# Where the rotated halves of queries and keys come from, and how one projection unit waits for its weights, in a two-layer decoder trunk

## The reference, cut to what matters

```python
for l in range(2):                      # SEQ 256, D_MODEL 1024
    p = rms_norm(x, mix_norm[l]) @ w_in[l]      # columns: RWKV-7 | conv | attention
    y = concat(rwkv7_mix(p_rwkv), short_conv_mix(p_conv), dilated_attention_mix(p_attn))
    x = x + y @ w_o[l]
    x = x + (dense SwiGLU if l == 0 else top-2-of-8 expert SwiGLU)(rms_norm(x))

def rope(x):                            # on normalised queries and keys, 6 heads of 64
    x1, x2 = x[..., :half], x[..., half:]       # half = 32
    return concatenate([x1 * cos - x2 * sin, x2 * cos + x1 * sin])
```

## Time and profile before

| | |
|---|---|
| timed runs | 1595.31, 1606.4 and 1609.2 us; median 1606.4 |
| span of the profiled execution | 1595.9 us; no other time is given for it |
| PE busy | 1563.6 us, 98% |
| DVE busy | 1268.4 us, 79% |
| ACT busy | 1072.2 us, 67% |
| POOL busy | 68.2 us, 4% |
| mean granted clock of PE | 0.995 of full |
| projection of layer 0 and of layer 1 | about 12 to 100 us and 445 to 535 us of the span |

### The profile page before, as it was taken

One profiled execution on the slowest core, in us unless ns is written; L12 is line 12 of the kernel. 1 busy time (PEld: TensorE's weight loads), 2 busy tenths in 40 slices (PEclk: granted clock), 3 DMA queues, 4 the chain that ended last, 5 costly groups with the idle time before them and its releaser, 6 DMA issues.

```text
span 1595.9 us, 29200 instructions
## 1 busy us (share of the span) xinstructions
PE 1563.6 (98%) x11204; PEld 1367.8 (86%) x11204; DVE 1268.4 (79%) x1446; ACT 1072.2 (67%) x1321; POOL 68.2 (4%) x72
## 2 busy tenths in 40 slices
PE   8989999999999999999999999999999999999998
PEld 8978999999999788788888888888888888888886
DVE  5676654544556867899999999999999999999996
ACT  5445354444455454788888888888888888888885
POOL 0012000000000210000100100000100000000000
PEclk9999899999999999999999999999999999999999
DMA  8500555555435006999999999999999999999994
GB/s 311 212 2 4 185 185 185 184 185 183 142 117 183 3 3 246 339 379 370 376 395 370 377 391 367 385 392 365 374 396 371 385 392 364 381 393 368 386 379 162
DMA packets 189562, 446.28 MB, mean 280 GB/s; under 512 B 8080, under 2 KB 10656, under 8 KB 189344
## 3 DMA queue, kind: packets, MB, share of 16 engines
q1 hardware_dynamic: 186480, 434.52, 74.5%
q0 software_dynamic: 2304, 7.87, 2.1%
q10 hardware_dynamic: 688, 2.62, 0.5%
HBM read 438.69 MB, written 6.29 MB: 279 GB/s over the span
## 4 chain that ended last, share of the span: by engine, by line
PE 93%; DVE 4%; ACT 1%; DMA 1%; issue 1%; POOL 0%; SPq 0%; DVEq 0%; ACTq 0%; POOLq 0%
PE bank L767 27%; PE bank L769 27%; PE bank L768 27%; PE bank L748 9%; PE bank L1437 2%; ACT w_hi L1515 1%; PE bank L788 0%; DMA ring<-in_w_in 0%; PE bank L1396 0%; PE bank L1177 0%; DMA ring<-in_dense_wg 0%; PE bank L938 0%; DVE w_lo L2198 0%; DVE ring L2021 0%; DVE w_lo L1945 0%
## 5 line engine op out<-in xcount | busy, mean ns | idle before, releaser
L1515 ACT ACTIVATE w_hi<-ring 128x1024 fp32r<-128x1024 f32 x812 | 858.6, 1061 | 330.9 <-PE bank L769 321.3
L2198 DVE TENSOR_TENSOR w_lo<-ring,w_hi 128x1024 fp32r<-128x1024 f32 x672 | 814.0, 1224 | 67.2 <-ACT w_hi L1515 17.5
L767 PE MATMUL bank<-w_hi,acts_hi 128*128 128x512 f32 (+1 forms) x1376 | 540.4, 393 | 2.3 <-DVE w_lo L2198 2.3
L769 PE MATMUL bank<-w_hi,acts_lo 128*128 128x512 f32 (+1 forms) x1376 | 533.8, 388 | 0.0
L768 PE MATMUL bank<-w_lo,acts_hi 128*128 128x512 f32 (+1 forms) x1376 | 533.2, 387 | 0.0
L767 PEld LDWEIGHTS bank<-w_hi,acts_hi 128*128 128x128 f32 x1376 | 258.8, 188 | 53.8 <-DVE w_lo L2198 3.4
L769 PEld LDWEIGHTS bank<-w_hi,acts_lo 128*128 128x128 f32 x1376 | 258.6, 188 | 53.3
L768 PEld LDWEIGHTS bank<-w_lo,acts_hi 128*128 128x128 f32 x1376 | 259.0, 188 | 50.0
L767 PE MATMUL bank<-acts_hi,w_hi 128*128 128x256 f32 x884 | 254.3, 288 | 3.4 <-DVE acts_lo L2105 1.7
L769 PE MATMUL bank<-acts_hi,w_lo 128*128 128x256 f32 x884 | 251.7, 285 | 0.0
L768 PE MATMUL bank<-acts_lo,w_hi 128*128 128x256 f32 x884 | 251.7, 285 | 0.0
(11 more groups left out here) (236 smaller groups left out, 1093.2 us busy)
## 6 DMA issues: line engine op xcount, KB each, us to landing
ring<-in_moe_wg SPq DMA_DIRECT2D x112, 1024.0 KB, 6.7
ring<-in_moe_wu SPq DMA_DIRECT2D x112, 1024.0 KB, 7.0
ring<-in_moe_wd SPq DMA_DIRECT2D x112, 1024.0 KB, 6.7
ring<-in_w_in SPq DMA_DIRECT2D x24, 1024.0 KB, 7.4
ring<-in_dense_wg SPq DMA_DIRECT2D x14, 1024.0 KB, 5.2
ring<-in_dense_wu SPq DMA_DIRECT2D x14, 1024.0 KB, 5.1
ring<-in_dense_wd SPq DMA_DIRECT2D x14, 1024.0 KB, 4.9
ring<-in_w_o SPq DMA_DIRECT2D x8, 1024.0 KB, 5.2
```

The lines of the kernel that those rows point to most:

```text
L767: pe.matmul(out_, a_hi, b_hi, start=first, stop=False, **kw)
L769: return pe.matmul(out_, a_lo, b_hi, start=False, stop=final, **kw)
L1515: return act.activation(o, i, ACT.Copy, **kw)
L2198: TT(w_lo[:, q, :], raw, w_hi[:, q, :].bitcast(F32), ALU.subtract).then_inc(lo_ready, 1)
```

## The change

Three things change. The constant matrix `rot` is gone and its sign goes into the table `sin`. `turn_heads` on PE is gone; instead POOL waits for `hs_used` and issues four transfers from SBUF to SBUF, each of 32 partitions by six tiles, which write the swapped halves into `sq_qk`; DVE waits for all four (`swapped_in`) and multiplies `sq_qk` with `sin` in place, in one instruction. And in `project` the first unit of chunk 1 no longer waits for all four pieces before it begins, but for each piece ahead of the products that need it.

```diff
-for _name, _n in (("ident", P), ("ones", P), ("pair", P), ("rot", P), ("cos", T), ("sin", T), ("strict", C),
+for _name, _n in (("ident", P), ("ones", P), ("pair", P), ("cos", T), ("sin", T), ("strict", C),
...
-    put("sin", np.sin(ang))
+    put("sin", np.where(i % HD < HD // 2, -1.0, 1.0)[:, None] * np.sin(ang))
...
+            def swap_halves(l):
+
+                pool.wait_ge(hs_used, 2 * l + 1)
+                for r0 in range(0, P, HD):
+                    for a, b in ((r0, r0 + HD // 2), (r0 + HD // 2, r0)):
+                        pool.dma_start(sq_qk[a:a + HD // 2, :, :], pT[b:b + HD // 2, 16:22, :]).then_inc(swapped_in, 16)
+
             for l in range(L):
 
+                swap_halves(l)
                 pool.wait_ge(unit_done, SINGLE0[l] + SINGLE[l])
...
-                if first and ch in SPLIT_IN:
-                    pe.wait_ge(lo_ready, IN0[l, ch] + 4)
-                elif first:
+                if first and ch not in SPLIT_IN:
...
+                    if first and ch in SPLIT_IN and k % 2 == 0:
+                        pe.wait_ge(lo_ready, IN0[l, ch] + k // 2 + 1)
...
-                def turn_heads():
-                    pe.wait_ge(hs_used, 2 * l + 1)
-                    for i in range(6):
-                        last = mm(bank[5 + i // 2][:, i % 2 * T:i % 2 * T + T], const("rot"), pT[:, 16 + i, :])
-                    last.then_inc(rot_done, 1)
-
...
-                HOOKS = {2: {1: lambda: head_spread(2 * l, 6, (5, 6, 7)), 3: turn_heads}, 0: {1: lora_wa, 3: lora_gv}}
+                HOOKS = {2: {1: lambda: head_spread(2 * l, 6, (5, 6, 7))}, 0: {1: lora_wa, 3: lora_gv}}
...
-                dve.wait_ge(rot_done, l + 1)
-                for i in range(3):
-                    TT(sq_qk[:, 2 * i:2 * i + 2, :], bank[5 + i][:, :].rearrange("p (i t) -> p i t", i=2),
-                       spread(const("sin"), 2), ALU.mult)
+                dve.wait_ge(swapped_in, 64 * (l + 1))
+                TT(sq_qk, sq_qk, spread(const("sin"), 6), ALU.mult)
```

More of the change, by code:

```diff
@@ L78, in constant_tables @@
     put("pair", i[:, None] // HD == i[None, :] // HD)
[L80 to L86, removed]
     inv_freq = np.float32(10000.0) ** (-np.arange(HD // 2, dtype=np.float32) * np.float32(2.0) / np.float32(HD))
@@ L367, in decoder_trunk @@
         rw_ready = sem("rw_ready")
-        rot_done = sem("rot_done")
+        swapped_in = sem("swapped_in")
         rope_ready = sem("rope_ready")
```

## The result

The changed kernel takes 1612.96 us (median of 14 runs, 1604.15 to 1625.19). The kernel before, run beside it, takes 1597.59 (14 runs, 1593.17 to 1609.82); the three runs that the prediction had, with their median of 1606.4, lay high. The ratio is 1.0090, with a 95% interval of 1.0067 to 1.0113: the change makes the kernel slower by about 15 us. No change was forecast, so the prediction was wrong, although the time lies just inside its range and the 0.9% within the 1% that it gave a chance of 0.94: the loss is clear of the noise, and its mechanism was not the one forecast.

A forecast was written before the change was run, and what follows sets the result against it. PE, busy 98% of the span, was taken as the bound, with DVE and the transfers nearly level around the rotation. Terms 0 + 0.9 - 0.9 = 0.0 us on 1595.9, put on the median: 1606 us, range 1595 to 1613.

The forecast's parts named there:

- T: Time from `hs_used` to the landing of the swap's last transfer; taken as 6.5 us in layer 0, 7.5 in layer 1.
- the level: The T at which a layer is as fast as before: 6.5 us in layer 0, 6.6 in layer 1.
- landing part: Within T, last issue to its landing: taken as 2.5 us in layer 0, 3.5 in layer 1; bounds 1.8 to 6.3.
- its traffic: Swap's 0.79 MB in the weight queues: 2 us of stream, cost put at 0, up to 2 us per layer without cover.
- The blocked writing of descriptors: DVE's two-port mode stops GpSimd writing descriptors: T up to 2.4 us longer, both layers 4.8; chance 0.02 within the slower-side rival.
- B: Rival at the swap: slow POOL issues and landing behind the weight stream, T = 11, +8 us, 1614; chance 0.15.
- C: Clock rival: the new PE wait at `lora_wa` brings 4 to 10 us at half clock, about +5, 1611; chance 0.15.
- part 2: First unit of chunk 1 waiting piece by piece: PE's 0.92 us idle goes in layer 0, 0 in layer 1.

The follow-up runs named there:

- held stream: Changed kernel, with SP holding back the weights of chunk 3 and all behind it until the swap's transfers have landed: 1598.02 us, ratio 0.9986.
- one copy: Changed kernel with one transfer over 128 partitions, same bytes, in place of four over 32; halves not exchanged, so rotation left out: 1610.52 us, measured once.
- two unread DVE products: Kernel before, rotation on PE, plus two DVE products of 768 columns that nobody reads, ahead of the rotation's sum: 1608.01 us, ratio 1.0069.
- The filler: Changed kernel plus 17 float32 PE products of 256 columns that nobody reads, in front of the wait in `lora_wa`: 1608.93 us, ratio 1.0070.
- ACT's issue: Changed kernel with the same four transfers issued by ACT instead of POOL, behind its second split of chunk 0: 1612.89 us, ratio 1.0080.
- half bytes: Changed kernel with the four transfers carrying the queries alone, the keys' halves left out: 1615.5 us, measured once.
- part 1 alone: Changed kernel with the piece-by-piece wait of chunk 1's first unit undone, one wait for all four pieces again: 1615.45 us, ratio 1.0116.

## Why the prediction was wrong

**The time it was put on.** The sum was made against the profiled execution and put on a median of three, 1606.4, that further runs bring to 1597.6. With a right sum the time would have been 9 us too high; that the result fell inside the range owes to this, and is luck.

**The shape was right.** The swap replaces 2.6 us of PE work by a wait; DVE waits for the DMA, PE waits in `lora_wa`, and each us of T above the level is a us of path in each layer. The run with the held stream shows the level: T of 6.5 and 6.4 at most gives a ratio of 0.9986.

**The term that was mis-sized is T, in its landing part.** The issue was taken at 4.0 us and measured 2.25 with 0.69 before it in layer 0, 2.05 with 0.30 in layer 1; the landing behind the end of the last issue was taken at 2.5 and 3.5 and measured 8.4 and 8.6. For four copies of 0.79 MB the choice leaned on a stream of 0.67 of the engines in layer 0 and one that "runs out at 490" in layer 1. But the swap itself fills what the stream leaves free: it added 3.8 us of full engines in layer 0, and the prediction put its traffic at 2 us, as a cost to the weights only and not to itself. The excess over the level, 4.9 + 4.4, is 9.3 us.

**The Trainium skill on the transfer.** "DMA: Bandwidth & Descriptors", section "Anatomy of one DMA", gave an estimate of 3.8 us for these 0.79 MB. The trace disagrees: 62.75 - 52.10 = 10.7 from the first issue to the last landing, and even with the stream held T was 6.5. The gathers' rows were the better guide; the low end of their landing, with their median issue, had given T = 11, though by luck in its parts: issue 7.2 and landing 3.8. The blocked writing of descriptors that rival B set beside itself is not seen, since POOL's four issues took 2.25 and 2.05 us in all, the length of one of its longer gathers.

**B and C came together.** B, a T of 11, was priced at +8 and given 0.15; C, a clock that falls behind the new wait, at +5 and 0.15. They were weighed as separate cases. They go together: in the single profiles the stretch at half clock that begins in the wait or within 3 us behind it is 3.4 us long in both layers where PE idles 2.6 us (held stream), 6.8 in both where it idles 3.5 (one copy), and 10.2 in both where it idles 7.2 and more (changed). Only the kernel with two unread DVE products is out of line, with 6.8 and 3.4 us for 1.75 and 2.07 of idling. Together B and C read 13; measured are 15. The run of the changed kernel with the clock at 0.993 took 1604.15, 7.2 above the median of before at 0.9938; that is near B, 9.3 less 1.0 of part 2. Its median is 8.8 above that run, with the mean clock at 0.9864; that is C. The filler bears the split out roughly: with before's clock the loss is 11 to 12 us with the longer T of that run, 4 us less than without.

**C was priced too low.** The prediction counted half of a stretch of 4 to 10 us, in one layer or both. In the profile after there are three such stretches near the waits, 27 us in all, of which about 6 lie in the idling itself, so some 10 us are lost, against 1.7 of before's one; the two unread DVE products, with 2 us of idling per layer, cost 7.6 us beyond their path.

**Part 2 was right**: 0.98 us in layer 0 against 0.92 forecast, nothing in layer 1.

**Open.** A stretch of 20 us at half clock, from 655.6 us in the changed kernel, stands also in the profiles of the one with ACT's issue, of the half bytes and of the single copy. It is not in the one profile of before, nor in that of part 1 alone, whose ratio is 1.0116, so the loss does not need it. No wait of the swap is near it. It begins behind a PE wait that both kernels have, before and changed, here with the windows behind it:

```profile
641.13 0.50 PE L767 MATMUL bank<-w_hi,acts_hi 128*128 128x512 f32 x1 [2.08 <-DVE w_lo L2198]
...
641.00:661.00 20.00, 19.87 (x105) 17.03 (x106) 16.42 (x20) 12.95 (x15) 2.53 (x3) 1.00 0.88 304
```

```profile
654.94 0.50 PE L768 MATMUL bank<-w_hi,acts_hi 128*128 128x512 f32 x1 [2.08 <-DVE w_lo L2193]
...
656.00:676.00 20.00, 20.00 (x65) 17.01 (x64) 8.65 (x13) 5.28 (x5) 1.38 (x3) 0.50 0.51 174
```

The kernel before has runs of 1608 to 1610 us, the size that such a stretch costs, so it may have such stretches too; they were not traced. Whether the change makes them more frequent was not settled, and a part of the 8.8 us may lie there. That the landing is set by what the 16 engines have ahead of them rests on sums of shares, which are 2.2 us short for the four copies, not on the order of single packets.

## What to carry to other kernels

Price a transfer that replaces work at its landing in its own stretch, the load of the DMA engines with the transfer itself in it, and do not take four copies over 32 partitions for one over 128. Where the engine that loses the work is the bound and cannot start something else, its freed time is idle time, and in the kernel with two unread DVE products 2 us of idle PE in each of two places cost 11 us by the medians (6.5 to 15.5 by the interval). It is no fixed price: in the kernel with the held stream 2.6 us in each, in the place of work taken away, cost nothing that the measurement can tell. If a step becomes late, look in both queues: taking the wait out of `lora_wa` only moved it from 60.6 to 64.9 us, to the next split, and only moving the step on DVE as well took it away.

## What the runs showed of the hardware

An idle of 2 us can be followed by some us at half clock, 1.2 GHz, and need not be. In the kernel with two unread DVE products the window 62 to 66, with the idle of 1.75 us in it, has 0.95 and the one from 66 to 70 has 0.50. Behind the wait of 2.08 us in the router part the kernel before had 1.00 for 20 us and the changed kernel 0.50. The clock fell in the idle itself where that was 7 us long (0.64 from 64 to 68). The mean clock of single runs of the changed kernel lay between 0.977 and 0.993, and their spans between 1623.4 and 1602.4 with it: most of the scatter of this kernel is the clock.

The kernel without six short float32 products per layer and without a PE wait in their place had a mean clock of 0.9907 against 0.9938 of before, and 0.9938 again with unread ones at their place. With 12 runs each this is a sign and no proof.

Four copies inside SBUF, each over 32 partitions, added 3.8 us of full DMA engines to the stretch, one copy of the same 0.79 MB over 128 partitions 2.0; by their own queue's rows it is 3.2 and 2.3 in layer 0, 3.2 and 2.0 in layer 1. The Trainium skill, "SBUF — State Buffer", section "Door 1: The DMA port swizzle", says that a transfer's rate depends on how many of 16 ports its partitions reach; by its mapping 32 in a row reach half of them. The trace agrees in direction: the factor is 1.9 by the sums, 1.4 and 1.6 by the queue's rows, where half the ports would make an estimated 2.

The idle of 2.6 us in the kernel with the held stream, where it takes the place of the removed products, goes with stretches of about 3.4 us at half clock in both layers, and yet that kernel's mean clock is that of before (0.9922 and 0.9916), whose profile has one of that length in layer 1 too.
